# A tenth weight slot, a split startup, and two conditioning groups moved to GpSimd in a two-layer latent backbone

## The reference

```python
for i in range(DEPTH):                       # DEPTH = 2
    sh_m, sc_m, g_m, sh_f, sc_f, g_f = split(silu(c) @ ada_w[i] + ada_b[i], 6)
    hx = modulate(x, norm_mix[i], sh_m, sc_m)        # rmsnorm * (1 + scale) + shift
    if i == 0:                                       # latent attention, 8 heads, 768 keys
        q_lat, kv_lat, k_rope = split(hx @ mla_w_in)            # 384, 256, 64
        q  = rope(rmsnorm(rmsnorm(q_lat) @ w_qb))               # 192 a head: 128 + 64 rotary
        k, v = keys_values(kv_lat, k_rope), the context's (hc @ mla_w_in[:, 384:]) ahead
        x = x + g_m * (softmax(q k^T * scale) v @ mla_w_out)
    else:                                            # short gated convolution
        b, cg, val = split(hx @ conv_w_in, 3)
        x = x + g_m * ((b * conv3(cg * val)) @ conv_w_out)
    # expert choice: each of 16 experts takes its 64 best tokens
    x = x + g_f * ec_moe(modulate(x, norm_ffn[i], sh_f, sc_f), router_w[i], w_gate, w_up, w_down)
```

## Time and profile before

| | us |
|---|---|
| median of 3 runs | 1654.43 (1653.51 to 1654.61) |
| the profiled execution's own time | 1655.29 |
| its span, first to last instruction | 1653.5 |
| TensorE busy | 1499.3 (91%) |
| VectorE busy | 542.5 (33%) |
| ScalarE busy | 234.0 (14%) |
| GpSimd busy | 73.3 (4%) |
| mean DMA rate | 305 GB/s |

### The profile page before, as it was taken

The page is one execution under the profiler, slowest core; times in us unless marked ns, Lnnn a source line. Parts: engine busy times, 40 slices in busy tenths (PEclk is TensorE's granted clock), DMA queues, the critical chain, the costliest instruction groups (busy, mean ns, idle before and its releaser), DMA issues.

```text
span 1653.5 us, 15124 instructions
## 1 busy us (share of the span) xinstructions
PE 1499.3 (91%) x6382; PEld 628.7 (38%) x6382; DVE 542.5 (33%) x976; ACT 234.0 (14%) x426; POOL 73.3 (4%) x58
## 2 busy tenths in 40 slices
PE   4999999998969999988988899999499999989897
PEld 2555555554423333332332344444133333333232
DVE  1255464541632323232322321113522323222232
ACT  3133343332400000000000200003200000000000
POOL 0010010100010000000000040000000000000000
PEclk9999999999979999999999999999699999999999
DMA  9441513496269999999999923030599999999997
GB/s 377 134 182 73 204 67 137 155 389 283 111 268 429 425 428 426 428 426 426 428 427 428 390 86 134 18 138 40 204 412 427 426 427 427 427 427 426 428 427 300
DMA packets 56061, 504.90 MB, mean 305 GB/s; under 512 B 7631, under 2 KB 7854, under 8 KB 25018
## 3 DMA queue, kind: packets, MB, share of 16 engines
q1 hardware_dynamic: 51744, 490.68, 71.7%
q0 software_dynamic: 2752, 8.92, 1.5%
q10 hardware_dynamic: 1498, 4.33, 0.7%
HBM read 497.62 MB, written 6.29 MB: 305 GB/s over the span
## 4 chain that ended last, share of the span: by engine, by line
PE 65%; DMA 28%; DVE 4%; ACT 2%; issue 1%; ACTq 0%; DVEq 0%; POOLq 0%
PE ps L802 24%; PE ps L883 10%; DMA ring<-in_exp_w_up_dram 7%; DMA work<-in_exp_w_up_dram 7%; PE ps L697 6%; DMA work<-in_exp_w_gate_dram 5%; DMA ring<-in_exp_w_gate_dram 5%; PE ps L816 3%; PE ps L461 3%; PE ps L613 3%; PE ps L572 3%; PE ps L388 2%; PE ps L511 2%; PE ps L515 2%; PE ps L599 1%; PE ps L576 1%
## 5 line engine op out<-in xcount | busy, mean ns | idle before, releaser
L802 PE MATMUL ps<-ring,work 128*64 128x512 f32 x2016 | 452.8, 598 | 38.9 <-DMA ring<-in_exp_w_gate_dram 15.8
L802 PEld LDWEIGHTS ps<-ring,work 128*64 128x64 f32 x2016 | 140.9, 137 | 331.5 <-issue 275.4
L802 PE MATMUL ps<-work 128*64 128x512 f32 x1056 | 239.1, 601 | 22.8 <-DMA work<-in_exp_w_gate_dram 8.5
L1534 DVE TENSOR_TENSOR work<-ps,work 128x1024 f32<-128x1024 f32 x120 | 141.4, 1220 | 288.3 <-PE ps L816 288.3
L802 PEld LDWEIGHTS ps<-work 128*64 128x64 f32 x1056 | 74.0, 138 | 176.8 <-issue 145.1
L816 PE MATMUL ps<-work 64*128 64x512 f32 x480 | 119.2, 615 | 0.0
L1100 ACT ACTIVATE work<-ps 128x512 f32<-128x512 f32 x32 | 19.1, 597 | 510.3 <-PE ps L802 510.3
L1552 DVE SCALAR_TENSOR_TENSOR work<-ps,gate_e,gate_ffn 128x512 f32<-128x512 f32 x32 | 24.0, 752 | 185.8 <-PE ps L802 185.8
L1545 DVE TENSOR_TENSOR work<-work,ps 128x512 f32<-128x512 f32 x32 | 22.0, 688 | 189.4 <-issue 157.2
L883 PE MATMUL ps<-ring 128*128 128x512 f32 x192 | 82.6, 592 | 0.0
L883 PE MATMUL ps<-ring,work 128*128 128x512 f32 x192 | 82.6, 592 | 0.0
(11 more groups left out here) (247 smaller groups left out, 1184.4 us busy)
## 6 DMA issues: line engine op xcount, KB each, us to landing
ring<-in_exp_w_up_dram SPq DMA_DIRECT2D x42, 2048.0 KB, 33.8
ring<-in_exp_w_down_dram SPq DMA_DIRECT2D x42, 2048.0 KB, 37.3
ring<-in_exp_w_gate_dram SPq DMA_DIRECT2D x42, 2048.0 KB, 32.1
ring<-in_ada_w_dram SPq DMA_DIRECT2D x22, 2048.0 KB, 8.1
work<-in_exp_w_gate_dram SPq DMA_DIRECT2D x22, 2048.0 KB, 34.5
work<-in_exp_w_up_dram SPq DMA_DIRECT2D x22, 2048.0 KB, 33.8
work<-in_exp_w_down_dram SPq DMA_DIRECT2D x22, 2048.0 KB, 34.3
ring<-in_conv_w_in_dram SPq DMA_DIRECT2D x3, 2048.0 KB, 38.7
```

Of the source, the lines that this page charges most:

```text
L802: last = mm(PS[64 * h:64 * h + 64, bank, :], lhsT[:, m * P + 64 * j:m * P + 64 * j + 64], slot_rows[sl][:, m, h * BANK:(h + 1) * BANK], st ...
L1534: v.tensor_tensor(row, PS[:, b:b + 2, :], row, ALU.add).then_inc(added[L], 1)
```

## The change

- **A tenth slot** for expert weights, in `W` from column 20480. Temporaries become smaller or shared for it: one buffer of router rows instead of two, one of gathered rows instead of two, SiLU and product in one buffer, the router lists elsewhere. Before the experts ten blocks are loaded; block n waits for block n - 10. Slot order and the regions of `R[0]` and `R[2]` change places.
- **Two copying engines at startup**: the eight latent groups are modulated by ScalarE (even) and VectorE (odd). Context transposes and their modulation come behind the first two low-rank products. The low-rank weight comes in two halves.
- **Two of the five later conditioning groups on GpSimd**: 16 slices of 1 MB. GpSimd multiplies each by its row of the condition, one number per partition (4 operations of 512 columns), and adds it to a sum of the group (4 more, but for the first slice of a group). TensorE then needs only a sum over partitions (`acc_collect`). Twelve units are left on TensorE: six in pair 2 and six in the last pair, none before.
- **Rotation and rotary keys on VectorE**: GpSimd's part of `turn_q` and the scaled rotary keys are done by VectorE.
- `top` leaves the maximum in PSUM.
- **Early row load**: the residual rows are issued ahead of the first six expert blocks, all of which now come after the last values product.

```diff
+    SUMMED = 2
+    SLICES = SUMMED * KC
-    UNITS = (len(GROUPS) - 1) * KC // 2
+    UNITS = (len(GROUPS) - 1 - SUMMED) * KC // 2
...
-        SLOT_AT = [(W, 0), (W, SLOT), (W, 2 * SLOT), (R[1], SLOT), (R[0], 0), (R[0], SLOT), (R[1], 0), (R[2], 0), (R[2], SLOT)]
+        SLOT_AT = [(W, 0), (W, SLOT), (W, 2 * SLOT), (R[1], SLOT), (R[2], 0), (R[2], SLOT), (R[1], 0), (R[0], 0), (R[0], SLOT), (W, 20480)]
+        ORDER = [list(range(10)), [6, 7, 8, 0, 1, 2, 3, 4, 5, 9]]
...
-        UNITS_IN = [3, 4, 4, 4, 5]
-        UNIT_AT = [sum(UNITS_IN[:n]) for n in range(len(UNITS_IN))]
-        UNIT_BANK = [0, 1, 2] + [7] * 12 + [7, 6, 7, 7, 7]
+        UNIT_AT = [0, 0, 0, 0, 6]
+        UNIT_BANK = [7] * 7 + [6] + [7] * 4
...
+            def load_slice(n):
+                L, part = GROUPS[1 + n // KC]
+                k = n % KC
+                sp.dma_start(ada_slice[n % 2], ada_w[L, k * P:(k + 1) * P, part * GROUP:(part + 1) * GROUP]).then_inc(ada_in[n % 2], 16)
+
             sp.wait_ge(ada_main, FIRST_LOADS)
+            load_slice(0)
+            load_slice(1)
             sp.dma_start(w_kvb, mla_w_kvb[0].rearrange("(k p) n -> p k n", p=P)).then_inc(whead_in, 16)
             sp.dma_start(w_qb, mla_w_qb[0].rearrange("(k p) n -> p k n", p=P)).then_inc(whead_in, 16)
-            sp.wait_ge(lat_done, NT)
-
+            for n in range(2, SLICES):
+                sp.wait_ge(slice_added, n - 1)
+                load_slice(n)
+            sp.wait_ge(ada_sum, 1 + SUMMED)
...
+                    if L == 0 and n == SLOTS - 1:
+                        sp.wait_ge(x_new[0], 2 * XT)
+                        sp.wait_ge(ada_sum, len(GROUPS))
...
-            sp.wait_ge(proj, 10 * PAIRS)
-            load_chunk(0, 0)
-            load_chunk(0, 1)
             for h, done in ((0, mixw_in[0]), (1, out_half_in)):
                 sp.wait_ge(unit_mm, UNITS - 1 + h)
                 sp.dma_start(mla_out[h], mla_w_out[0, :, h * BANK:(h + 1) * BANK].rearrange("(k p) n -> p k n", p=P)
                              ).then_inc(done, 16)
-            sp.wait_ge(krs_ready, PAIRS)
-            load_chunk(0, 2)
-            sp.wait_ge(trn, 8 * PAIRS)
-            sp.wait_ge(pv_done, HEADS - 2)
-            load_chunk(0, 3)
             sp.wait_ge(pv_done, HEADS)
             sp.dma_start(acc, x[0].rearrange("(t p) d -> p t d", p=P)).then_inc(xres_in, 16)
-            load_chunk(0, 4)
-            load_chunk(0, 5)
+            sp.wait_ge(krs_ready, PAIRS)
+            for n in range(6):
+                load_chunk(0, n)
...
+            def acc_collect(c):
+
+                part = GROUPS[c][1]
+                total = ada_acc[c % 2]
+                pe.wait_ge(slice_added, KC * c)
+                for g in range(4):
+                    cols = total[:, g * BANK:(g + 1) * BANK]
+                    n, half = (4 * part + g) // 2, g % 2
...
+                last.then_inc(ada_sum, 1)
...
                 if ahead:
-                    project(i + 1, 0, u)
+                    units = (lambda *ns: [unit(n) for n in ns]) if i == 2 else (lambda *ns: None)
...
-                    pe.wait_ge(unit_added, KC // 2 * (i + 1))
-                    ada_collect(i + 1)
+                    if i < SUMMED:
+                        acc_collect(i + 1)
+                    else:
+                        pe.wait_ge(unit_added, KC // 2)
+                        ada_collect(i + 1)
                     values(1)
-                    unit(u + 3)
+                    units(5)
                 else:
-                    unit(u)
-                    unit(u + 1)
+                    unit(6)
+                    unit(7)
                     scores(1)
                     probs_T(0)
-                    unit(u + 2)
+                    unit(8)
                     scores(2)
                     probs_T(1)
-                    unit(u + 3)
+                    unit(9)
                     scores(3)
                     probs_T(2)
-                    unit(u + 4)
+                    unit(10)
                     values(0)
+                    unit(11)
...
-            for g in range(KC, 12):
+            for g in range(1, KC, 2):
+                dve.wait_ge(inT, g + 1)
+                v.tensor_scalar(hT[:, g, CX:KEYS], PS[:, T_BANKS[g % 6], :], scl[0][0][:, g, 0:1], modv[0][0][:, 0, g, 0:1],
+                                ALU.mult, ALU.add).then_inc(inT_d, 1)
...
-                v.tensor_tensor(qr, qr, rope_gain[:, 0:1, :].to_broadcast([P, 8, ROPE]), ALU.mult).then_inc(qg_ready, 1)
-                dve.wait_ge(qg_ready, n + 1)
+                own.link(v.tensor_tensor(qr, qr, rope_gain[:, 0:1, :].to_broadcast([P, 8, ROPE]), ALU.mult))
                 q5 = qr.rearrange("p t (a b f) -> p t a b f", a=2, b=2)
                 o5 = q_rot.rearrange("p t (h n) -> p (t h) n", h=2).rearrange("p t (a b f) -> p t a b f", a=2, b=2)
                 c8 = [rope_cs[:, m].rearrange("p t (a f) -> p t a f", a=2) for m in range(2)]
-                t8 = [rtmp[m].rearrange("p (t a f) -> p t a f", a=2, f=RF) for m in range(2)]
+                t8 = [r.rearrange("p (t a f) -> p t a f", a=2, f=RF) for r in rtmp]
                 v.tensor_tensor(t8[0], q5[:, :, :, 0, :], c8[0], ALU.mult)
-                own.link(v.tensor_tensor(t8[1], q5[:, :, :, 1, :], c8[1], ALU.mult))
-                v.tensor_tensor(o5[:, :, :, 0, :], t8[0], t8[1], ALU.subtract).then_inc(qrot_d, 1)
+                v.tensor_tensor(t8[1], q5[:, :, :, 1, :], c8[1], ALU.mult)
+                v.tensor_tensor(t8[2], q5[:, :, :, 1, :], c8[0], ALU.mult)
+                own.link(v.tensor_tensor(t8[3], q5[:, :, :, 0, :], c8[1], ALU.mult))
+                v.tensor_tensor(o5[:, :, :, 0, :], t8[0], t8[1], ALU.subtract)
+                v.tensor_tensor(o5[:, :, :, 1, :], t8[2], t8[3], ALU.add).then_inc(q_turned, 1)
...
-                v.reciprocal(smal[:, 32:52], smal[:, 32:52]).then_inc(rk_ready, 1)
-                dve.wait_ge(rk_ready, n + 1)
+                own.link(v.reciprocal(smal[:, 32:52], smal[:, 32:52]))
                 kk = kvtoks[n % 2].rearrange("p t (h n) -> p (t h) n", h=2)[:, :, 0:NOPE]
                 v.tensor_tensor(kk, kk, smal[:, 32:44].unsqueeze(2).to_broadcast([P, 2 * NT, NOPE]), ALU.mult).then_inc(kn_ready, 1)
+                v.tensor_tensor(kr_s.rearrange("p t (h n) -> p t h n", h=2),
+                                krot.unsqueeze(2).to_broadcast([P, NT, 2, ROPE]),
+                                smal[:, 32:44].rearrange("p (t h) -> p t h", h=2).unsqueeze(3).to_broadcast([P, NT, 2, ROPE]),
+                                ALU.mult).then_inc(krs_ready, 1)
...
-                    own.link(v.tensor_reduce(stat[:, 66 + j:67 + j], PS[:, 2 * j:2 * j + 2, 0:SCR], AX.XY, ALU.max))
-                    v.tensor_tensor(stat[:, 64 + j:65 + j], stat[:, 66 + j:67 + j], smal[:, 52 + 2 * t + j:53 + 2 * t + j],
+                    most = PS[:, 2 * j, SCR:SCR + 1]
+                    own.link(v.tensor_reduce(most, PS[:, 2 * j:2 * j + 2, 0:SCR], AX.XY, ALU.max))
+                    v.tensor_tensor(stat[:, 64 + j:65 + j], most, smal[:, 52 + 2 * t + j:53 + 2 * t + j],
...
-            own = Chain(pool, pool_step)
-            pool.wait_ge(krot_ready, 1)
-
-            def pair(i):
-                pool.wait_ge(qg_ready, i + 1)
...
-                pool.wait_ge(rk_ready, i + 1)
-                g.tensor_tensor(kr_s.rearrange("p t (h n) -> p t h n", h=2),
-                                krot.unsqueeze(2).to_broadcast([P, NT, 2, ROPE]),
-                                smal[:, 32:44].rearrange("p (t h) -> p t h", h=2).unsqueeze(3).to_broadcast([P, NT, 2, ROPE]),
-                                ALU.mult).then_inc(krs_ready, 1)
-
-            for i in range(PAIRS):
-                pair(i)
+            pool.wait_ge(setup_out, 1)
+            for n in range(SLICES):
+                c, k = 1 + n // KC, n % KC
+                part, total = ada_slice[n % 2], ada_acc[c % 2]
+                pool.wait_ge(ada_in[n % 2], 16 * (n // 2 + 2))
+                for q in range(4):
+                    cols = slice(q * BANK, (q + 1) * BANK)
+                    last = g.tensor_tensor((part, total)[k == 0][:, cols], part[:, cols], cond_T[:, k, 0:1].to_broadcast([P, BANK]),
+                                           ALU.mult)
+                if k >= 1:
+                    last.then_inc(slice_scaled, 1)
+                    pool.wait_ge(slice_scaled, n - n // KC)
+                    pool.wait_ge(slice_added, n)
+                    for q in range(4):
+                        cols = slice(q * BANK, (q + 1) * BANK)
+                        last = g.tensor_tensor(total[:, cols], part[:, cols], total[:, cols], ALU.add)
+                last.then_inc(slice_added, 1)
...
-                    if e >= 2:
-                        pool.wait_ge(xs_T[L], e - 1)
-                    g.indirect_dma_start(out=xs[:, s, :], out_offset=None, in_=xn_half,
+                    if e >= 1:
+                        pool.wait_ge(xs_T[L], e)
```

(31 more changed lines are left out.)

269 lines of the change are left out of this document (141 added, 128 removed).

## The result

The changed kernel takes **1668.13 us** (median of 4 runs, 1667.87 to 1668.49) against 1654.52 for the kernel before in the same comparison: a ratio of 1.0081, 95% interval 1.0063 to 1.0098. It is 13.6 us slower. The forecast was 1657 in a range of 1630 to 1668; the median lies at its upper end, 11 us above the forecast. The profiled execution took 1667.87 us, its span is 1665.7.

What follows compares the result with a forecast made beforehand. The weight stream was taken to bound the experts, with TensorE close, and TensorE's chain to bound attention. Terms from startup to tenth slot summed to +2.7 us on 1655.3, 1658.0, forecast as 1657 us; range 1630 to 1668.

Steps and rivals of the forecast that it cites:

- Startup, low-rank, setup: Up to pair 0's first scores: startup -3.5, low-rank +2.4, setup of pair 0 +13.1 and +3 by the clock.
- third rival: Setup and pair 0: TensorE's gaps keep the clock at 1.2 GHz, up to 8 us more, 1666; chance 0.07.
- the 3 us for the clock: Setup of pair 0: longer TensorE gaps leave the clock at 1.2 GHz in more of it, +3 us.
- The lock: Attention: VectorE operations with two SBUF inputs, or TENSOR_SCALAR SBUF to SBUF, wait for GpSimd's running operation, about 1.1 us each.
- the rival without a lock: Low-rank to pair 0: no lock that matters, -31.7 us, 1623; chance 0.10.
- Reductions: VectorE reductions of SBUF data beside GpSimd: taken as not waiting; with the other bound +10 us in all.
- Pair 0: Attention pair 0: four units go, but rotation and locked norms come onto the path; +3, and +1.5 by the clock.
- pair 1: Attention pair 1: GpSimd through, four units gone, `acc_collect` costing what the collection did; -7.6 us.
- the ring: Expert weights in both layers: ten blocks ahead instead of nine, each later block landing 4.91 us earlier; -9.8 us.
- Pairs 2 and 3: Attention pairs 2 and 3: six and six units for four and five, plus 0.7 us before a copy; +6.4 us.
- row load: Output stage: residual rows land before the first sum, TensorE's 4.13 us wait goes, products behind run faster; -5.8 us.
- Tenth slot: Experts of both layers: every later block lands 4.91 us earlier, smaller buffers cost nothing; -9.8 us.

Runs made afterwards that it cites:

- Experiment 1: Changed kernel with nearly all of GpSimd's arithmetic left out (14 of 16 slices get one product and one sum of 2 columns): 1634.8 us.
- experiment 2: Changed kernel with GpSimd's products and sums cut into operations of 128 columns instead of 512, same arithmetic: 1658.7 us.
- Experiment 4: Changed kernel with the collection as four products of a matrix of ones by the sum, a VectorE copy and four transposes: 1656.7 us.
- experiment 9: Kernel before with only the residual rows issued directly after the last values product, ahead of expert blocks 2 to 5: 1648.9 us.
- experiment 8: Changed kernel with the tenth slot kept but every expert block issued one step later, so nine blocks are ahead: 1677.7 us.
- experiment 10: Changed kernel with the conditioning groups back on TensorE, GpSimd idle in attention, all else of the change kept: 1634.3 us.
- experiment 7: Changed kernel with nearly all of GpSimd's arithmetic left out and the collection by four products of ones, a copy and four transposes: 1622.9 us.

## Why the prediction was right in part

**Startup, low-rank, setup (+15.0 forecast, +12.3 measured).** The low-rank products start 5.65 us earlier, as forecast, and wait 2.62 us for VectorE. `turn_krot` takes 9.4 us (9.7 forecast), `turn_q` 8.9 (9.4), the gaps are 6.3 and 4.3 (6.9 and 6.6). (The terms that I gave for `turn_krot` add up to 9.6, and the third rival's 8 us on top of 1657 to 1665, not 1666.) Only the 3 us for the clock did not appear as a sum of their own; half clock is there, beside waits that hide it.

**The lock** was priced right. Experiment 1 takes 33.4 us away, and I had 34 between the forecast and the rival without a lock. The turn is one operation of GpSimd, experiment 2 shows it by its size. GpSimd was to end near 205 and ended at 200.

**Reductions.** I took them as not waiting. They took 0.95 us beside GpSimd throughout, as without it. The Trainium skill (SBUF — State Buffer, section Who interferes with whom) has them never contending with GpSimd, and the trace agrees.

**Pair 0 (+4.5, measured +10.4) and pair 1 (-7.6, measured -3.0): the step that failed.** I wrote that "`acc_collect` costs what the collection did", without pricing its products: a product of one column still loads 128x128 weights in two records of 0.23 us each, and there are eight. The collections take 6.0 and 5.7 us; the one written as before takes 2.3. The values behind them took 8.19 and 5.98 us instead of 5.35, at half clock. The kernel before had 2.3 and 1.7 us for the two collections and 5.34 and 5.45 for the values behind them, so the rows give 6.5 us of error in pair 0 and 4.6 in pair 1; by the stages it is 5.9 and 4.6. Experiment 4 puts other products in their place and gives 11.4 us, 2.0 of them ahead of the collection. That this is also the distance between forecast (1657) and result (1668) is in part chance: the other errors, -2.7 us in the setup, +1.5 in the ring, +0.6 and -0.3, nearly cancel, and 1 us lies between the profiled executions and the medians.

**Pairs 2 and 3 (+6.4, measured +7.0), row load (-5.8, measured -6.1)** came as forecast; experiment 9 gives the row load alone 6.0.

**Tenth slot (-9.8, measured -8.3).** The rule is right: experiment 8 finds 9.8 us between nine and ten blocks ahead (4.7 + 5.1), and in experiment 10 the experts are 5.4 and 4.4 us shorter than before, 9.8 in all. Of the 1.5 us missing in the changed kernel, about 1 in layer 0 can be the transposes ahead of the convolution: their clock was granted at 0.50 from 948 to 951, and in the profile of experiment 8 at 1.00. With nine blocks, though, the experts are 0.5 and 1.0 us longer than before's, and I had put the single buffers and the rest at nothing. Whether they cost that was not separated; it is within what one profile can tell.

**The rivals.** "No lock" had the right time for its case: 1622.9 measured in experiment 7, 1623 forecast. The clock that stays down was a mechanism of the right kind in the wrong place: I looked for it behind TensorE's gaps, and it cost most behind products with almost no columns. What I did not weigh at all was the choice itself. With every turn taken away and the old collection, the move of two groups gives 1622.9 against 1634.3 with the groups on TensorE: in this order of the other work it could bring 11 us at most, and its turns cost 33.

## What to carry to other kernels

Before work goes from TensorE to GpSimd, count the VectorE operations that run at the same time with two SBUF inputs, or that scale or copy from SBUF to SBUF, and charge each one GpSimd operation; if the move is made, cut GpSimd's operations small. Price each new product by its records and its weight load, not by its columns, and look at the clock of what stands behind it. Where parts of a change are independent, sum them apart: here startup, row load and tenth slot together gave 20 us, and the move to GpSimd took them back and 14 more.
